# Hymba block on one core: three projection tiles in turn on halves of ada_w, w_out copied from step 10 on, rank scans with zeros in PSUM as second operand

## What is computed

```python
mod = silu(c) @ ada_w + ada_b                       # 1024 x 3072
shift, scale, gate = split(mod, 3)
h = rmsnorm(x, norm_g) * (1 + scale) + shift
z = h @ w_in                                        # xr, gr, q, k, v, ga, qi, ki, wi
xr = causal_depthwise_conv(xr, conv_w, conv_b)      # width 4, 512 channels
y_r = rg_lru(xr, ...) * silu(gr)                    # gates, h[t] = a[t] h[t-1] + u[t]
score = sum over 8 index heads of relu(qi . ki / 8) * wi        # causal
idx = top_k(score, 256)
y_a = softmax attention of q (8 heads of 64) over the keys in idx, * silu(ga)
out = rmsnorm(x + gate * (concat(y_r, y_a) @ w_out), final_g)
```

## Time and profile before

| | |
|---|---|
| runs | 621.46, 621.24, 619.52 us; median 621.24 |
| the profiled execution's own time | 619.93 us |
| its span (first to last instruction) | 618.1 us |
| mean granted TensorE clock over the span | 0.926 |
| busy: PE / DVE / ACT / POOL | 535.4 / 439.5 / 377.4 / 233.5 us |
| head, to the first projection matmul | 0 to 45.1 us |
| tiles 0, 1 and part of 2 | 45.1 to 85.2 |
| index scores | 85.2 to 162.8 |
| search beside projections | 162.8 to 353.4 |
| threshold to mask, first attention steps | 353.4 to 397.0 |
| attention and output projection | 397.0 to 618.1 |

### The profile page before, as it was taken

How to read it: one execution, slowest core, us unless ns; L and a number is a source line. 1 busy time by engine, 2 the same in 40 slices (tenths; PEclk the granted TensorE clock), 3 DMA queues, 4 the chain that set the end, 5 groups by cost and what they waited for, 6 DMA issues and landing times.

```text
span 618.1 us, 8029 instructions
## 1 busy us (share of the span) xinstructions
PE 535.4 (87%) x2676; PEld 444.8 (72%) x2676; DVE 439.5 (71%) x992; ACT 377.4 (61%) x679; POOL 233.5 (38%) x195
## 2 busy tenths in 40 slices
PE   1459989998999999999999526489999999999994
PEld 1346868777787777778888415478889999888873
DVE  5987386885999889898697886854475666664522
ACT  6513236453499999987898555554466666656531
POOL 5150862352344274677642003740402030313322
PEclk9859999998999999999999855569999999999999
DMA  8967342430112111135550420110011000101011
GB/s 335 418 206 266 105 118 53 102 85 18 36 34 69 34 36 34 35 103 137 140 133 0 177 96 0 68 36 2 8 61 43 28 36 34 41 30 69 0 69 68
DMA packets 16457, 51.96 MB, mean 84 GB/s; under 512 B 4000, under 2 KB 5024, under 8 KB 15392
## 3 DMA queue, kind: packets, MB, share of 16 engines
q1 hardware_dynamic: 16416, 51.45, 26.3%
HBM read 37.81 MB, written 4.19 MB: 68 GB/s over the span
## 4 chain that ended last, share of the span: by engine, by line
PE 68%; DVE 11%; DMA 7%; POOL 5%; ACT 4%; issue 3%; SPq 2%; DVEq 0%; POOLq 0%; ACTq 0%
PE pair L1373 30%; PE pair L1470 13%; PE pair L1492 6%; PE pair L1505 5%; DMA ada<-in_ada_w 4%; PE pair L1448 3%; PE pair L1449 2%; DMA qs<-half_lo 2%; PE pair L1422 2%; DVE rank L1156 2%; PE pair L1514 2%; PE pair L1413 2%; PE pair L1414 2%; DVE tie L1158 1%; POOL half_lo L726 1%
## 5 line engine op out<-in xcount | busy, mean ns | idle before, releaser
L1373 PE MATMUL pair<-h_hi,w_hi 128*128 128x512 f32 (+1 forms) x352 | 114.4, 407 | 1.6 <-DVE h_lo L1064 1.5
L1373 PE MATMUL pair<-h_lo,w_hi 128*128 128x512 f32 (+1 forms) x352 | 109.8, 393 | 0.0
L1373 PE MATMUL pair<-h_hi,w_lo 128*128 128x512 f32 (+1 forms) x352 | 109.0, 391 | 0.0
L1298 DVE TENSOR_TENSOR pt_lo<-pair,pt_hi 128x512 fp32r<-128x512 f32 (+3 forms) x96 | 50.5, 554 | 71.1 <-ACT pt_hi L963 70.5
L858 ACT ACTIVATE bias_sb<-score_sb,tinies 128x1024 bf16<-128x1024 f32 (+2 forms) x93 | 95.7, 1032 | 3.2 <-DVE tinies L1109 3.1
L696 POOL TENSOR_SCALAR w_hi<-w_raw 128x1024 fp32r<-128x1024 f32 (+1 forms) x22 | 29.4, 1339 | 136.3 <-PE pair L1373 120.5
L1373 PEld LDWEIGHTS pair<-h_hi,w_hi 128*128 128x128 f32 (+1 forms) x352 | 65.0, 188 | 19.0 <-issue 6.2
L1373 PEld LDWEIGHTS pair<-h_lo,w_hi 128*128 128x128 f32 (+1 forms) x352 | 66.0, 188 | 15.5 <-issue 0.8
L1373 PEld LDWEIGHTS pair<-h_hi,w_lo 128*128 128x128 f32 (+1 forms) x352 | 65.6, 186 | 15.4 <-issue 0.7
L1095 DVE TENSOR_SCALAR_CACHE_REDUCE bias_sb<-score_sb,tinies 128x640 bf16<-128x640 f32 (+2 forms) x93 | 72.6, 802 | 0.9
L781 POOL TENSOR_TENSOR x_res<-q_free,x_res 128x512 f32<-128x512 f32 x14 | 18.1, 1296 | 121.0 <-DVE q_free L1269 121.0
(11 more groups left out here) (195 smaller groups left out, 1254.2 us busy)
## 6 DMA issues: line engine op xcount, KB each, us to landing
w_raw<-in_w_tiles SPq DMA_DIRECT2D x21, 512.0 KB, 3.5
ada<-in_ada_w SPq DMA_DIRECT2D x8, 1024.0 KB, 18.4
x_sb<-in_x SPq DMA_DIRECT2D x8, 512.0 KB, 7.1
ada_g<-in_ada_w SPq DMA_DIRECT2D x8, 512.0 KB, 4.5
qs<-half_hi SPq DMA_DIRECT2D x16, 256.0 KB, 3.6
qs<-half_lo SPq DMA_DIRECT2D x16, 256.0 KB, 4.4
wo_raw<-in_w_out SPq DMA_DIRECT2D x8, 512.0 KB, 6.4
x_res<-in_x SPq DMA_DIRECT2D x8, 512.0 KB, 3.3
```

What stands on the lines that cost most here:

```text
L1298: nc.vector.tensor_tensor(pt_lo[:, 4 * b:4 * b + nc4, hh, :], psum[use % 2][:, 0:nc4 * P].rearrange("p (c q) -> p c q", q=P), f32(pt_hi[:, ...
L1373: ins = nc.tensor.matmul(psum[banks[half]][0:width, :], w[b][:, k, 0:width], hh[:, k, half * HALF:(half + 1) * HALF], start=(k == 0 and p ...
```

## The change

It has three parts.

1. **The head and the slabs.** The groups are k = 0 to 3 and 4 to 7. `ada[k]` becomes two halves, one for each group, loaded by 16 DMAs with pieces of 2 KB: all first halves, between the loads of x's tiles 4 to 7, then slabs 0, 1 and 2, then all second halves. There are three PSUM pairs and four slab buffers for the first tiles, later two pairs and three buffers (`PROJ_PAIR`, `SLAB_BUF`). ACT's copies of the transposes stand between its squares. `modulate(k)` on ACT makes both `h_hi` and the full value from `xt` by an activation with scale and bias; DVE and, for k = 2 and 3, POOL take the difference. PE runs tiles 0, 1 and 2 in turn on the blocks of group 0, sums group 1's columns, and goes on. The planner starts from other free times (`FIRST_US` by engine), with tiles 0 to 2 already under way, so every list of `ORDER` changes. The transposes of wi come after tile 2. A slab's load waits for the tile that last used its buffer instead of for a split. A convolution also waits for the gate matmuls before it.
2. **w_out.** `WO_START` is 10 instead of 5.
3. **Rank scan.** The scan in `mask` adds a column of zeros in PSUM, broadcast, where it added the tie row a second time; its start value and the factor 0.5 behind it are adapted, so that ranks are counted once, not twice. `prepare` writes the column once.

```diff
-MOD_GROUPS = [(0, 3), (3, KC)]
+MOD_GROUPS = [(0, KC // 2), (KC // 2, KC)]
+LO_POOL = (2, 3)
...
+SLAB_BUF = {w: w if w < 4 else (w - 1) % 3 for w in range(NW)}
...
+FIRST = 3
+PROJ_PAIR = {j: j if j < FIRST else (j + 1) % 2 for j in range(NJ)}
...
-WO_START = 5
+WO_START = 10
...
-FIRST_US = 46.0
+FIRST_US = dict(PE=30.0, ACT=55.0, DVE=56.0, POOL=42.0, SP=40.0)
+FIRST_STEP_US = (3.46, 0.1, 0.6)
...
+        need = [("kstep", SLAB_TILE[SLAB_PREV[w]], KC - 1)]
...
-    add("PE", ("wi",), 0.9, 1, ("evac", 0), ("kstep", 1, KC - 1))
+        add("POOL", ("split", w), SPLIT_US, 5, (("load", w), 5.0))
+    add("PE", ("wi",), 0.9, 1, ("evac", 0), ("kstep", FIRST - 1, KC - 1))
...
+        if u == 1:
+            need.append(("evac", FIRST - 1))
...
-        _pair = 2 + _o[1] % 2 if _o[0] == "idx" else 2
+        _pair = 3 - _o[1] % 2 if _o[0] == "idx" else 2
...
-                if w >= 2:
-                    sp.wait_ge(w_split, w - 1)
+                if w == FIRST:
+                    sp.wait_ge(xt_ps, 2 * KC)
+                if SLAB_PREV[w] is not None:
+                    sp.wait_ge(proj_done, SLAB_TILE[SLAB_PREV[w]] + 1)
...
+                load_ada(k, 0)
+                if k < NT // 2:
+                    load_x(NT // 2 + k)
+                if k == NT // 2:
+                    load_slab(0)
+            load_slab(1)
+            load_slab(2)
+            for k in range(KC):
+                load_ada(k, 1)
+            load_slab(FIRST)
...
-            split_slab(0)
-            split_slab(1)
+            for w in range(FIRST):
+                split_slab(w)
+            for k in LO_POOL:
+                pool.wait_ge(h_full, k + 1)
+                nc.gpsimd.tensor_tensor(h_lo[:, k, :], xt[:, k, :], f32(h_hi[:, k, :]), ALU.subtract).then_inc(h_lo_pool, 1)
+            split_slab(FIRST)
...
+            def modulate(k):
+                act.wait_ge(mod_ok, k // (KC // 2) + 1)
+                act.wait_ge(xt_act, KC + k + 1)
+                shift, scale = mod[:, k:k + 1], mod[:, 8 + k:9 + k]
+                nc.scalar.activation(h_hi[:, k, :], xt[:, k, :], ACT.Identity, bias=shift, scale=scale).then_inc(h_hi_ok, 1)
+                act.wait_ge(h_hi_ok, k + 1)
+                nc.scalar.activation(xt[:, k, :], xt[:, k, :], ACT.Identity, bias=shift, scale=scale).then_inc(h_full, 1)
+            for t in range(NT):
+                square(t)
+                if t >= NT // 2:
+                    copy_xt(2 * (t - NT // 2))
+                    copy_xt(2 * (t - NT // 2) + 1)
+            for u in range(KC, KC + 6):
+                copy_xt(u)
+            modulate(0)
+            copy_xt(KC + 6)
+            copy_xt(KC + 7)
+            for k in range(1, KC):
+                modulate(k)
...
+            for t in range(NT // 2):
+                normalize(t)
             for k in range(KC):
...
+                accumulate(k, 0)
+                if k < NT // 2:
+                    normalize(NT // 2 + k)
+            modulation(0)
+            accumulate(0, 1)
+            accumulate(1, 1)
+            low_half(0)
+            accumulate(2, 1)
+            accumulate(3, 1)
+            low_half(1)
+            for k in range(KC // 2, KC):
+                accumulate(k, 1)
+            modulation(1)
+            for k in range(KC // 2, KC):
+                low_half(k)
...
+                link(nc.vector.memset(zero_ps, 0.0))
...
-                link(nc.vector.tensor_tensor_scan(rank[i][:, :], tie[i][:, :], tie[i][:, :], float(2 * n - 4 * TOPK), ALU.add, ALU.add))
-                link(nc.vector.tensor_scalar(cols(c, nK), rank[i][:, n - 1:n], 0.5, cols(c, cnt), ALU.mult, ALU.subtract))
+                link(nc.vector.tensor_tensor_scan(rank[i][:, :], tie[i][:, :], zero_ps.to_broadcast([P, n]), float(n - 2 * TOPK), ALU.add, ALU.add))
+                link(nc.vector.tensor_scalar(cols(c, nK), rank[i][:, n - 1:n], cols(c, cnt), 0.5, ALU.subtract, ALU.mult))
...
+                            dve.wait_ge(slot_done, SLOT["gates", ct - 1, 1] + 1)
...
+                for p, (w, hh) in enumerate([(w_high, h_lo)] if low else [(w_high, h_hi), (w_low, h_hi)]):
+                    for half in range(2):
+                        ins = nc.tensor.matmul(psum[proj_ps[PROJ_PAIR[j]][half]][0:width, :], w[:, k, 0:width], hh[:, k, half * HALF:(half + 1) * HALF],
+                                               start=(k == 0 and p == 0 and low == 0), stop=(k == KC - 1 and low == 1))
...
-            for k in range(KC):
-                kstep(0, k)
-                if k >= KC // 2:
-                    kstep(1, k - KC // 2)
+            def first_two(k):
+                for low in range(2):
+                    for j in range(2):
+                        first_part(j, k, low)
+            def third(k):
+                for low in range(2):
+                    first_part(2, k, low)
+            for u in range(KC + 6):
+                transpose_x(u)
+            mod_sums(0)
+            for u in range(KC + 6, 2 * KC):
+                transpose_x(u)
+            first_two(0)
+            first_two(1)
+            third(0)
+            first_two(2)
+            third(1)
+            first_two(3)
+            third(2)
+            mod_sums(1)
+            third(3)
             for k in range(KC // 2, KC):
-                kstep(1, k)
+                first_two(k)
+            for k in range(KC // 2, KC):
+                third(k)
```

More of the change, by code:

```diff
@@ L40 @@
 BIG = 3.0e38
-MOD_GROUPS = [(0, 3), (3, KC)]
+MOD_GROUPS = [(0, KC // 2), (KC // 2, KC)]
+LO_POOL = (2, 3)
+LO_DVE = [k for k in range(KC) if k not in LO_POOL]
 SEARCH_BITS = 31
@@ L245, in stages @@
         before = [c]
-    free = dict(PE=FIRST_US, ACT=FIRST_US, DVE=FIRST_US, POOL=0.0, SP=0.0)
+    free = dict(FIRST_US)
     end = {}
@@ L583, in f32, with wait_low, slab_use @@
             return ap.bitcast(F32)
+        def wait_low(engine, k):
+            if k in LO_POOL:
+                engine.wait_ge(h_lo_pool, LO_POOL.index(k) + 1)
+            else:
+                engine.wait_ge(h_lo_ok, LO_DVE.index(k) + 1)
+        def slab_use(w):
+            return sum(SLAB_BUF[v] == SLAB_BUF[w] for v in range(w + 1))
         block = ctx.enter_context(nc.Block())
@@ L613, in _ @@
             for o in ORDER["SP"]:
-                if o[0] == "load" and o[1] >= 2:
+                if o[0] == "load":
                     load_slab(o[1])
```

194 lines of the change are left out of this document (103 added, 91 removed).

## The result

The changed kernel takes 631.74 us (median of 4 runs, 630.14 to 632.37), before 621.07 (4 runs): ratio 1.0173, 95% interval 1.0146 to 1.0200. It is **slower by 10.7 us**, or 1.7%; 618.2 was forecast, within 610 to 626. Its profiled execution took 630.14 with a span of 628.4, so the forecast has to be held against 630.1.

The account below looks back on a forecast made before the run. PE, filled by projections, and a chain of scores, counting search and masks were taken to bound the kernel. From 619.9, +6.0 - 14.4 + 11.9 - 6.8 + 1.5 = -1.8 gave 618.1 (618.2 given), range 610 to 626.

Parts of the forecast that it names:

- first index matmul: Start of the index scores: wi and POOL's splits delay it from 85.2 to 86.8 us, 1.6 later.
- index phase: Index scores: ACT waits for stacks before evacuating qi 2 and qi 3; +4.4 us on 77.6, bounds 0 and +11.
- scores to search end: Threshold search after the scores: -14.4 up to kv's evacuation and +11.9 behind it.
- masks and w_out: Behind the search: -6.8 us from masks without POOL's wo_lo beside them, +1.5 from w_out copies returning later.
- DVE has those columns ready by 42.5: Head: DVE's sums for the second group are done at 42.5 us, before PE's column sums.
- the queue position on PE is the cost of the new head: Head: eleven steps ahead of the second group's sums on PE leave ACT idle from 39.7 to 50.3 us.
- rival B: PE standstills in head and index phase lower its clock, costing 7.5 us: 625.7 us; chance 0.20.
- the pair -14.4 and +11.9: Search: scores to kv takes 90 us for 104.2 (-14.4); steps and counts behind kv take 98.1 for 86.2 (+11.9).
- rival D: Reordering buys nothing: scores 6 us late, search as long as before, only masks gain; 620.6 us; chance 0.15.
- bound of -4.7: Rank scans in the masks: lower bound if all six scans, 9.4 us, halve; no change was forecast.
- rival C: Rank scans in the masks halve with the zero column in PSUM: 613.5 us; chance 0.03.
- bound of +2.1: Rank scans: upper bound, the excess that the scan of 768 showed beside POOL; no change was forecast.

Follow-up runs that it names:

- e11: e6 with all low halves of the head on DVE and group 1's column sums ahead of tiles 0 and 1's block 3 on PE; 617.31 us.
- e6: e5 with the planner counting 8 us more for an index tile's stacks to land, so ACT evacuates qi 2 and qi 3 later; 616.75 us.
- e5: The changed kernel with wi's transposes after tile 2's block 5 and slabs 4 and 5 split behind qi 0's low half; 622.86 us.
- e1: The kernel before with WO_START = 10 as its only edit; 615.45 us.
- e8: The kernel before with WO_START = 10 and the zero scans, without the new head and order; 614.79 us.

## Why the prediction was wrong

Its sum was 618.1 (618.2 given); the time to hold it against is 630.1. Its four terms against what was measured:

| | forecast | measured | miss |
|---|---|---|---|
| first index matmul | +1.6 | +8.0 | +6.4 |
| index phase | +4.4 | +6.2 | +1.8 |
| scores to search end | -2.5 | +2.5 | +5.0 |
| masks and w_out | -5.3 | -6.4 | -1.1 |

*Start of the scores: mechanism right, size wrong.* The first step that failed is the head, a term of the +1.6. "27.5" for group 0 on DVE was 30.3: the normalisations stood between sums and so ended at 23.2, and the four last sums took 1.79 each, where 1.24 was taken. That price came from a trace in which POOL had nothing to do until 33.1, as slab 0 landed only then. The change loads slabs 0 to 2 ahead of ada_w's second halves, POOL splits them from 22.8 on, and DVE's sums run beside that. The prediction priced the moved loads at nothing and did not ask what their earlier landing would start. (No run takes the splits away; that they cost the difference is read from the rows: in the same trace the sums ahead of 22.8 took 1.28.) The column sums took 3.57 at a granted clock of 0.50, where 1.8 was taken. The first h_hi was done at 36.3 for 31.2, 5.1 us late.

Then "DVE has those columns ready by 42.5" was wrong by 10: it was 52.9. Of these, 4.7 are the later start (DVE began the second group's sums at 34.9, forecast 30.2), and 5.0 are four sums that took 2.49 each beside POOL for 1.24. The prediction's bold sentence, that the queue position on PE is the cost of the new head, falls with it: DVE was ready only 0.9 us before PE came to the sums, and e11 shows that moving them gives nothing. PE itself needed 17.3 us from its first projection matmul to these sums, forecast 16.8, so it came late because it had started late. How much of kiwi's 6.4 us each part is worth stays open: in e6 a start 2.3 us earlier brought nothing, since DVE and POOL then met for longer. From kiwi's evacuation on, the forecast's distances fit: the first index matmul comes 24.3 us behind the end of kiwi's tile, forecast 24.3.

The larger lesson is what was taken as given. PE's 8.7 us of lead don't reach kiwi's tile, since PE now shares its time among three tiles: it ends at 68.9, 6.1 later than before. Then wi stands behind tile 2, and two splits ahead of the first low half. The prediction had priced both and asked nothing further. e5 shows that these places alone, with the head as slow as it is, are worth 8.9 us.

*Index phase.* The two waits of ACT came as forecast. The rest, 1.8 us, fits rival B's mechanism, the low clock behind such waits, though no run tests it alone: from 93.2 to 130 the granted clock was 0.86, where before it was 1.00 from 85.2 to 121.0 and 0.96 from there to 162.8.

*Search: the mechanism was wrong.* The second step that failed is the pair -14.4 and +11.9: PE's lead was to shorten the search up to kv, and the steps and counts behind kv were to give most of it back. "I take 90, against 104.2" was nearly right, 91.3 from the scores to kv. But the counts left out there came back behind kv, with more: 101.8 for the forecast 98.1 and the 86.2 of before.

That the forecast is no further off is luck. It has 56 projection steps behind kv and then 17 us from "the last evacuation at 336.5". But the 65.52 us of the earlier trace rows that end there are 48 steps, and the last evacuation of before stands eight steps further on:

```profile
347.36 1.02 ACT L841 ACTIVATE ga<-pair 128x1024 f32<-128x1024 f32 x1 [1.75 <-PE pair L1373]
```

So these eight steps are counted twice. The same sum made for before gives 267.2 + 98.1 = 365.3, where the search ended at 353.4: the +11.9 is this difference and holds no count. With 6.0 us behind the true last evacuation the sum behind kv is about 86, as before, and the whole forecast about 606. In the change 20.1 us passed from the start of the last evacuation, at 350.01, to the search's end. PE had nothing to do by then (0.45 us of the 20.0 from 350 to 370), while DVE was busy for 17.5.

Over all kernels run, the distance from scores complete to search end is 189.2 to 193.4, while its start moves by 15 us and kv by 12. That is rival D's sentence, "the search takes as long as before". DVE and ACT, which do the counts, were busy for 93.7 and 92.8 of 104.2 us in the earlier trace rows already. That they, and not PE, set the length of the search is the likely reading of that row and of the constant distance; no run shortens the counts to show it.

*Masks, w_out, scans: right.* For w_out -5.3 was forecast; e1 gives -4.9 for it alone, e8 -6.0 for both parts (614.79 against 620.75). Where the scans ran alone they kept their durations, 2.29 for 1024 elements and 2.02 for 896 in both traces. The bound of -4.7 and rival C are out, and so is any slowing. By the figures of the Trainium skill (VectorE: DVE Perf Modes, the TRN2 errata section), 120 fixed cycles from PSUM and 58 from SBUF, one would estimate 62 cycles more with a PSUM source; this pair of traces doesn't show it, with 2.29 before and after. What the prediction didn't see is that the zero scans have a worth of their own, 1.9 us, as long as POOL works beside the masks. Its bound of +2.1 (the excess of the scan of 768 beside POOL) came from the right row, but that excess was there to be gained, not to be added.

The range failed because its upper end was one rival's price, 625.7, while a late head, a longer phase and a search that gives nothing are three misses that can come together; they did.
